# Summing weighted decode values on TensorE in two rounded halves instead of in full float32

## The reference, cut to what matters

```python
def dilated_attention_step(q, k, v, cache, win, dil, rel_bias, h0):
    kv_all = jnp.concatenate([cache, jnp.stack([k, v], axis=2)], axis=1)
    idx = lc + jnp.arange(t)[:, None] - jnp.arange(n_keys)[None, :] * dil
    kvg = jnp.take(kv_all, jnp.maximum(idx, 0), axis=1)
    ...
    p, lse = softmax_weights(s, None)
    o = jnp.einsum('bhtj,btjhd->bthd', p.astype(v.dtype), kvg[:, :, :, 1])
```

## Time and profile before

| | |
|---|---|
| median of 3 runs (lowest, highest) | 1822.39 us (1822.28, 1822.65) |
| profiled execution, first to last instruction | 1823.3 us |
| mean granted PE clock | 0.972 of 2.4 GHz |
| PE busy | 1747.2 us, 96% |
| DVE busy | 995.4 us, 55% |
| ACT busy | 725.3 us, 40% |
| PE share of the chain that ended last | 77% |

### The profile page before, as it was taken

The page is one execution under the profiler, slowest core; times in us unless marked ns, Lnnn a source line. Parts: engine busy times, 40 slices in busy tenths (PEclk is TensorE's granted clock), DMA queues, the critical chain, the costliest instruction groups (busy, mean ns, idle before and its releaser), DMA issues.

```text
span 1823.3 us, 32494 instructions
## 1 busy us (share of the span) xinstructions
PE 1747.2 (96%) x12451; PEld 1660.6 (91%) x12451; DVE 995.4 (55%) x1389; ACT 725.3 (40%) x1054; POOL 156.4 (9%) x257
## 2 busy tenths in 40 slices
PE   8999999998999998999959999999999999999995
PEld 7999999766989896999959999999999999999995
DVE  4457667554377575666664444444444444444546
ACT  4343443353433232334344544443333333333333
POOL 1012222323010100000050000000000000000001
PEclk9999999897999998999979999999999999999997
DMA  6579999668688887677837878876775555556541
GB/s 217 155 267 315 324 321 342 164 180 256 223 301 298 306 290 233 220 228 252 254 128 237 256 246 265 250 230 213 259 224 165 167 161 161 165 167 200 163 155 52
DMA packets 204717, 410.75 MB, mean 225 GB/s; under 512 B 12220, under 2 KB 105686, under 8 KB 200416
## 3 DMA queue, kind: packets, MB, share of 16 engines
q1 hardware_dynamic: 178384, 254.41, 43.7%
q10 hardware_dynamic: 7488, 91.33, 15.0%
q0 software_dynamic: 18768, 63.94, 10.8%
HBM read 403.47 MB, written 94.92 MB: 273 GB/s over the span
## 4 chain that ended last, share of the span: by engine, by line
PE 77%; DVE 8%; DMA 7%; issue 4%; ACT 2%; POOL 1%; DVEq 0%; SPq 0%; ACTq 0%
PE bank L1289 74%; DMA VST<-in_cache_b_dram 3%; PE bank L1292 3%; DMA raw<-in_w_in_dram 3%; DVE wlo L898 1%; DVE PV L1091 1%; DVE PV L1094 1%; POOL U L572 1%; ACT L859 1%; DVE U L1205 1%; DVE U L1195 1%; DVE VST L1082 1%; ACT whi L615 0%; DMA xs_s<-in_x_sample_dram 0%; DVE VST L1085 0%
## 5 line engine op out<-in xcount | busy, mean ns | idle before, releaser
L898 DVE TENSOR_TENSOR wlo<-raw,whi 128x1024 fp32r<-128x1024 f32 x473 | 576.1, 1226 | 646.9 <-ACT whi L615 646.3
L615 ACT ACTIVATE whi<-raw 128x1024 fp32r<-128x1024 f32 x473 | 498.2, 1060 | 837.6 <-PE bank L1289 611.0
L1289 PE MATMUL bank<-X1H,whi 128*128 128x288 f32 x1408 | 420.1, 298 | 17.6 <-DVE X1L L1212 11.7
L1289 PE MATMUL bank<-X1L,whi 128*128 128x288 f32 x1408 | 417.4, 296 | 0.0
L1289 PE MATMUL bank<-X1H,wlo 128*128 128x288 f32 x1408 | 415.8, 295 | 0.0
L1289 PE MATMUL bank<-XH,whi 128*128 128x288 f32 x1248 | 375.1, 301 | 0.7 <-issue 0.5
L1289 PE MATMUL bank<-XL,whi 128*128 128x288 f32 x1248 | 369.9, 296 | 0.0
L1289 PE MATMUL bank<-XH,wlo 128*128 128x288 f32 x1248 | 368.6, 295 | 0.0
L1289 PEld LDWEIGHTS bank<-X1H,whi 128*128 128x128 f32 x1408 | 265.7, 189 | 21.5 <-issue 16.8
L1289 PEld LDWEIGHTS bank<-X1H,wlo 128*128 128x128 f32 x1408 | 267.0, 190 | 0.0
L1289 PEld LDWEIGHTS bank<-X1L,whi 128*128 128x128 f32 x1408 | 266.1, 189 | 0.0
(11 more groups left out here) (234 smaller groups left out, 1789.7 us busy)
## 6 DMA issues: line engine op xcount, KB each, us to landing
raw<-in_w_ffn_in_dram SPq DMA_DIRECT2D x176, 512.0 KB, 3.6
raw<-in_w_in_dram SPq DMA_DIRECT2D x156, 512.0 KB, 6.0
out_dram<-in_cache_b_dram ACTq DMA_DIRECT2D x28, 2336.0 KB, 10.9
raw<-in_w_ffn_out_dram SPq DMA_DIRECT2D x88, 512.0 KB, 4.1
KST<-in_cache_b_dram POOLq DMA_DIRECT2D x32, 512.0 KB, 5.1
QST<-tok_scratch POOLq DMA_DIRECT2D x32, 512.0 KB, 6.6
VST<-in_cache_b_dram POOLq DMA_DIRECT2D x16, 1024.0 KB, 12.9
raw<-in_w_out_dram SPq DMA_DIRECT2D x32, 512.0 KB, 5.3
```

Source lines behind the costliest of these rows:

```text
L615: nc.scalar.activation(whi[s][:, :], raw[s][:, :], ACT.Copy).then_inc(hi_done, 1)
L898: nc.vector.tensor_tensor(wlo[s][:, :], raw[s][:, :], whi[s][:, :].bitcast(F32), ALU.subtract).then_inc(lo_done, 1)
L1289: return nc.tensor.matmul(out, lhsT, rhs, start=start, stop=stop, **kw)
```

## The change

It replaces the four float32 matmuls of a sequence by eight fp32r matmuls, four with the rounded half of PV and four with the rest.

```diff
+        PVL = at("PVL", [P, DS, 512], 195328, F32R)
+        PVH = [at("PVH0", [P, 2, 512], R5 + 16384, F32R), at("PVH1", [P, 2, 512], R3 + 13824, F32R)]
+        ONECOL = at("ONECOL", [P, 2 * P - 1], 206336, F32R)
...
+            def values_high(b):
+
+                act.wait_ge(pv_ready, b + 1)
+                if not known_below(b, 1):
+                    act.wait_ge(pv_used, b)
+                nc.scalar.activation(PVH[0][:, :, :], PV[:, 0:2, :], ACT.Copy).then_inc(pvh_done, 1)
+                nc.scalar.activation(PVH[1][:, :, :], PV[:, 2:4, :], ACT.Copy).then_inc(pvh_done, 1)
+
             def gates(i):
                 copy_b3(i)
...
                     split(PH_GATE, i, k)
...
+                values_high(i)
                 for m in range(4):
                     src = tile(PH_GATE, i, m)
...
+            def values_low(n):
+
+                for hf in range(2):
+                    dve.wait_ge(pvh_done, 2 * n + hf - 1)
+                    nc.vector.tensor_tensor(PVL[:, 2 * hf:2 * hf + 2, :], PV[:, 2 * hf:2 * hf + 2, :],
+                                            PVH[hf][:, :, :].bitcast(F32), ALU.subtract).then_inc(pvl_done, 1)
+
             def gates(b, loads, par):
                 for k in range(8):
                     split(PH_GATE, b, k)
+                    if k == 0:
+                        values_low(b)
...
             gates(7, 4, 1)
+            values_low(DB)
...
-                pe.wait_ge(pv_ready, b + 1)
+                pe.wait_ge(pvl_done, 2 * b + 2)
                 for t in range(DS):
                     row = DS * b + t
-                    ins = mm(bank[6][0:NS, :], ONECOL[:, NS - 1 - row:2 * NS - 1 - row], PV[:, t, :],
-                             row == 0, row == NS - 1)
+                    one = ONECOL[:, P - 1 - row:2 * P - 1 - row]
+                    mm(bank[6][:, :], one, PVH[t // 2][:, t % 2, :], row == 0, False)
+                    ins = mm(bank[6][:, :], one, PVL[:, t, :], False, row == NS - 1)
```

More of the change, by code:

```diff
@@ L228, in build @@
         PV = at("PV", [P, DS, 512], 195328)
-        ONECOL = at("ONECOL", [P, 2 * NS - 1], 203776)
+        PVL = at("PVL", [P, DS, 512], 195328, F32R)
+        PVH = [at("PVH0", [P, 2, 512], R5 + 16384, F32R), at("PVH1", [P, 2, 512], R3 + 13824, F32R)]
+        ONECOL = at("ONECOL", [P, 2 * P - 1], 206336, F32R)
         OROW = at("OROW", [NS, 512], 204288)
@@ L309, in build @@
             sem("vp_done"), sem("pv_ready"), sem("pv_used"), sem("orow_done"), sem("os_ready"))
+        pvh_done, pvl_done = sem("pvh_done"), sem("pvl_done")
         cv_in = [sem("cv_in0"), sem("cv_in1")]; cv_used = sem("cv_used")
@@ L1066, in outputs_low @@
                         .then_inc(otl_done, 1)
-                nc.vector.memset(ONECOL[:, :], 0.0).then_inc(onecol_done, 1)
+                nc.vector.memset(ONECOL[:, :].bitcast(F32), 0.0).then_inc(onecol_done, 1)
                 dve.wait_ge(onecol_done, 1)
-                nc.vector.memset(ONECOL[:, NS - 1:NS], 1.0).then_inc(onecol_done, 1)
+                nc.vector.memset(ONECOL[:, P - 1:P].bitcast(F32), 1.0).then_inc(onecol_done, 1)
             def value_products(b, loads, par, step):
```

## The result

The changed kernel takes 1839.91 us in the median (1835.41 to 1844.61, four runs) against 1822.52 beside it: ratio 1.0093, 95% interval 1.0072 to 1.0113. It is slower, as forecast; but the 17.4 us are nearly three times the 6.0 of the forecast, and the time lies above the range, whose end was 1837.0.

What follows compares the result with a forecast made beforehand. PE was taken to bound a gate pass at 29.70 us; a delay of 17.6 us at pass 2, shrinking 0.5 in each of five passes, and the end gave +6.0: 1828.4 us, range 1820.5 to 1837.

Steps and rivals of the forecast that it cites:

- What bounds the kernel now: Gate stage: PE, busy without a break, bounds a pass at 29.70 us; PV becomes ready after ACT's first sigmoid.
- PE's saving: Decode part: eight one-pass matmuls take 1.85 us instead of 3.55, so a pass needs 28.0 us of PE.
- The first seam: Pass 0 to 1: ACT waits for PV ahead of the sigmoids, so PE starts pass 1 15.5 us late.
- The chain of a pass: Steady gate pass: ACT and DVE work to PV, copies and sigmoid make 29.2 us; PE stalls 1.2 us.
- The step that failed: Later passes: VST needed by 10.9 us (13.5 after PV) and 16.9 after PV; taken as not binding.
- Rival B: Later passes: transfers stay as late as now, VST 18.0 us after PV; six passes at 1.1 give 1835; 14%.
- The sign named for B: Later passes: DVE's first VST step waits for the transfer to 14 us or more after PV.
- Rival C: Later passes: the clock falls at each stall, losing 1.5 us; six times gives 1837.5 us; 10%.
- D: Later passes: PE stays the bound, PV comes 1.2 us sooner, a pass takes 28.0; 1821.2 us; 15%.
- E: First seam costs nothing because sigmoids are not held up; only PE's saving shows, 1809.5 us; 6%.
- The end: Last PV at 723.7: low half, two subtractions, sum 1.95, then 4.37 us to the merge stage at 733.6.

Runs made afterwards that it cites:

- a3: The kernel before with the eight one-pass fp32r matmuls alone, no halves made, each value counted twice: 1819.79 us, ratio 0.9973.
- a6: The changed kernel with ACT's PV copies behind the next pass's second high half, PE's decode part behind chunk 4, cache copy behind k = 4: 1811.71 us.
- a4: The changed kernel with ACT's cache copy issued behind high half k = 4 instead of at the head of the pass: 1825.70 us, ratio 1.0009.
- a8: As a6, but the last sequence summed in float32 from PV itself, without halves: 1808.11 us, ratio 0.9913 to the kernel before.

## Why the prediction was right in sign and wrong in size

- **What bounds the kernel now:** PE was the bound of a pass, and right under it lay PV. That held: a3 shows that the room under PE was almost nothing.
- **PE's saving:** 1.85 us for eight matmuls was 1.97, that is 0.2343 us from start to start for 512 columns and one longer first start. The upper of the two bounds (0.237) was the near one. The pass of 28.00 us in a6 equals the forecast's 28.0 although the sum is 0.12 longer than forecast; that is in part luck, and no run shows what makes it up. By the rule of the Trainium skill (TensorE: Matmul & The Clock Gate, section "Wait — 56ns, not 53.3ns?") the eight were estimated at 1.73 us; the trace does not agree here either.
- **The first seam:** forecast 15.5 us late and 34.9 from PV of sequence 0 to that of sequence 1 (548.5 - 513.64); measured a pause of 15.19, and 540.02 - 505.72 = 34.30. Right. Before, it was 536.35 - 513.64 = 22.71, so the seam costs 11.6 us of the 17.8 by which the stage grew.
- **The chain of a pass:** forecast 29.2 us with a stall of 1.2; a4, where no transfer holds it, has 29.13 and 0.91. The sum of nine durations was right to 0.1.
- **The step that failed** is the one that took the transfers as not binding: "Now the copy goes out 3.6 us after PV and one raw slot is freed instead of three, so I take VST as not binding". For VST itself it held: the first load came 5.7 to 6.1 us after it was issued, and though the second came 16.8 to 18.3 us after PV, DVE's list of waits has none for VST. But the raw chunk for the one slot that is freed right behind PV was put at nothing, though its low half stands ahead of the second VST step. By the forecast's own sum it had to land 14.6 us after PV (29.2 less 1.1, 1.2 and 12.3); it landed 15.4 to 17.6 after it. Put into the same sum, it gives the period: landing at 588.0 is 16.8 after PV (571.15); high half 1.1, low half 1.2, then step, low half, step, low half, step, low half and last step, 12.3: 31.4. The trace has 571.15 to 602.59, 31.44. From PV of sequence 1 to that of sequence 7 the trace has 187.5 where the forecast had 175.2: 12.3 us, about all that the forecast lacks.
- **Why the term was missed:** I let the copy go out 3.6 us behind PV, after ACT's copies and sigmoids. At the seam shown it goes out at 572.50, 1.35 us behind PV, while they are still running, beside the second VST load and the raw chunk, and all land together. The moment alone does not explain it: one seam earlier the copy went out 2.25 us behind PV, and both loads were as late (17.9 and 16.2 us behind PV). And that fewer freed slots would mean earlier landings was argued, not worked out in bytes. a4 shows that the copy beside them is what costs; how much later it must go out to do no harm was tried at k = 4 alone.
- **Rival B** had the mechanism right (transfers as the last to come), but through VST and at 1.1 us a pass, with the landings of before. The second VST load came 16.8 to 18.3 us after PV where it had come 15.8 to 18.1, the raw chunk 15.4 to 17.6 where it had come 12.9 to 16.0, and a pass cost 2.0 more than forecast (31.2 against 29.2). The sign named for B, a wait of DVE for VST to 14 us or more, missed it: the first VST step began at 582.54, 11.4 us after PV, without such a wait. B should have had more than 14% and a higher price.
- **Rival C** was half there: the clock fell for 3.41 us in three of the later passes (at 606.5, 668.0 and 698.7), behind pauses of 3.20, 2.58 and 2.49 us, but not behind 2.92. Since transfers, not PE, paced these passes, it is not shown that this cost time.
- **Rivals D and E** fell: PE waited for a sigmoid seven times, the first time for 15.19 us.
- **The end:** forecast 9.9 us from the last PV to the merge stage, measured 737.52 - 727.48 = 10.04. Right.

What stays open is which of the two transfers alone would hold the pass: the raw chunk ends ACT's wait in the trace, and the second VST load lands within 2 us of it in each pass. No run moves one without the other, and a4 moves the copy that delays both.

## What to carry to other kernels

Work that is put into an engine's fixed order must stand behind everything that others wait for and is ready sooner; here two copies of 1 us cost 17. In the stage 11.6 us of this arose at the first seam, where the wait for a late input stood ahead of four sigmoids that PE needs, and 6.8 in the six periods behind it (187.5 where before had 180.7), where transfers came late. When a change shifts when transfers are issued, sum the loop once more with every transfer that is freed at that moment, not only with the one that the changed lines name. And before an engine is made faster, look at which loop runs right under it: the one-pass matmuls alone gave a ratio of 0.9973 (a3), and the order of a8, with ACT's copies and a DMA that nothing in the stage waits for moved out of that loop's way, 0.9913.

## What was not expected of the hardware

- An ACT-queue DMA was issued while earlier ACT instructions were still running: at 572.50, ahead of the sigmoids at 573.10 that stand before it in ACT's order. In the kernel before, where ACT's last sigmoid waited for PE until 563.50, the issue came behind it, at 564.05.
- At the six later seams of the changed kernel the second VST load, the raw chunk and the cache copy started within 1.3 us of each other and took 13.5 to 17.1 us. The first VST load, as large as the second and issued 0.75 us ahead of it, took 5.7 to 6.1. In the kernel before the change, at whose seam of passes 2 and 3 the copy went out ahead of both VST loads, the first took 13.5 us there. A raw chunk that started when no VST load did, behind the last PV, took 3.8.
- The clock's state ahead of the gate stage, which the change does not touch, moved the profiled spans: of the 7.9 us by which PV of sequence 0 was earlier after the change, 3 lie in the windows with 0.52 and 0.84 granted over about the same work. The rest lies ahead of them, where 343 to 385 us had 0.88 before and 1.00 after. Together this is nearly half of what the change cost.
